# The GLA gate of a two-block fp32 kernel: tokens as the stationary operand, the bias as a rank-1 matmul, and four insertions moved

## The chip, the cores and the metric

The kernel runs on one core of one Trainium2 chip. The metric is the device time of one execution in microseconds (us); lower is better. TensorE (PE) has two rows in the profile, PE for matmuls and PEld for the loads of their stationary operand. VectorE is DVE, ScalarE is ACT, GpSimd is POOL and SyncE is SP.

## The reference, cut to what matters

The program is a stack of two blocks over 256 tokens of width 1024, all in fp32. The second block has two layers, and the change lies in the mixer of each of them. In a mixer the normed input is multiplied by `w_in`; 16 of the resulting columns, `p[..., o5:o6]`, are the input of a gate:

```python
h = rms_norm(x, norm_mix_g[l])
p = h @ w_in[l]
y_a = conformer_conv(p[..., :256], p[..., 256:512], ...)     # 31 taps
...
gate_logit = p[..., o5:o6] @ gla_gate_w[l] + gla_gate_b[l]   # [256, 16] @ [16, 256]
log_a = jax.nn.log_sigmoid(gate_logit) / 16.0
y_c = gla_chunked(q_c, k_c, v_c, log_a)                      # cumulative sums of log_a in chunks of 32
```

The convolution needs its own product, a sigmoid gate, a transpose to channels on partitions, and 31 taps for each of 2 channel tiles.

## The kernel before, in words

There are two token tiles of 128 (index m) and eight tiles of the width (index kt). All weights come as a stream of units of 128x2048 fp32 numbers through four slots. Each unit is split into two parts that TensorE can take at its fast rate: ACT writes the high part (`hi(U)`, L463, `whi<-raw`), DVE subtracts it and writes the low part (`lo(U)`, L872, `wlo`). The normed and transposed input is split likewise into `xth` and `xtl`. A product is then three matmuls (`split3`, L1404 to L1406). A slot comes free for the next DMA, which the SP queue issues, once `lo` of its unit is done, and `hi(U)` waits until TensorE has used unit U-4.

A mixer layer runs on TensorE as `step(0)` to `step(3)`, a half-width product (`mv`), `step(5)` and `out_product`. One step is for each m 24 matmuls of 512 columns (8 kt of 3). `step(1)` uses units U0+2 and U0+3, `step(2)` U0+4 and U0+5, `step(3)` U0+6 and U0+7; its second half of kt (kt 4 to 7) needs the second unit. Small work is inserted by hooks after a given kt of m=0 or m=1, or between the two (`end`). The order on each engine is written out by hand; engines wait on semaphores only.

The order around the change, between step 0 and step 3:

- **TensorE**: step 0; the gate product (24 matmuls, `ginh`/`ginl` stationary, `xth`/`xtl` of all 256 tokens moving, output 16x256, so already transposed); step 1 with `conv_turn` after kt 1 of m=0 (four transposes of `hc`, L1432) and `logits` after kt 3 of m=0 (L1749); step 2 with `cumsum` after kt 5 of m=0 (L1757) and `qk_turn` after kt 1 of m=1; step 3.
- **ACT**: sigmoid of the conv gate (L704), `gT` copy (L707), `hpad` copy (L711, from which the taps read), `hi(U0+4)`, then Abs, Exp and Ln of the logits (L717 to L721), `hi(U0+5)`, `gqk` (L727), `hi(U0+6)`, three reads of the cumulative sum (L737 to L739), `hi(U0+7)`.
- **DVE**: `hc` (L1165), two instructions that scale the logits and add the bias (L1169), taps 0 to 4 (L1185, L1189), `lo(U0+4)`, taps 5 to 8, the minimum and subtraction that finish `la` (L1199), `lo(U0+5)`, taps 9 to 13, `lo(U0+6)`, `dG` (L1208), `dec` (L1212), and so on to the last tap (41), the sum with POOL's part (L1262) and the seventh state (L1244).
- **POOL**: 20 taps of the second channel tile as product and sum (L431, L435), from `hpad` on.

Later on, TensorE waits for DVE twice in this layer by construction: the state products (L1789, `state_inc(n)`) need `state(n-2)`, and `ln_turn` (transposes of `cacc`) with the `gla_out` behind it needs the last tap and `state(6)`.

Of the kernel before, what the change touches and what calls it, by code (L numbers as in the profile page):

```python
# [77 lines left out]
def two_blocks_kernel(nc, x_in, stream, cols, bs_col, ws_t, gs_row, fin_row, fin2_row, rel_rows, ffn_cw,  # L78
                      conv_w, conv_ln, moba_g, gla_g, gate_w, gate_b, gate_in, out):
    ctx = ExitStack()  # L80
    with ctx:
        def sem(name):
            return ctx.enter_context(nc.semaphore(name))
# [3 lines left out]
        def at(name, shape, offset, dt=F32):  # L87
            return nc.alloc_sbuf_tensor_at(name, [P] + shape, dt, offset=base + 4 * offset)
# [26 lines left out]
        def const(name, shape, dt=F32):  # L115
# [69 lines left out]
        mqT = at("mqT", [2, SEQ], o_sa + 1792)  # L185
        mkT = at("mkT", [2, SEQ], o_sa + 2304)
        mv = at("mv", [M, 256], o_sa + 2816)
        gw_sb = at("gw_sb", [256], o_sb)
        gb_sb = at("gb_sb", [256], o_sb + 256)
        gin = at("gin", [KT * RANK], o_sb + 512)  # L190
# [41 lines left out]
        x_ltr, x_bn, x_ag, x_lms, x_lr, x_nrm, x_btr, x_sl = (  # L232
            sem("conv_ln_" + n) for n in ("transposed", "stats", "mean", "var", "rstd", "normed", "back", "silu"))
        x_ev = sem("mix_kept")
        x_gT, x_gTc, x_lg, x_z, x_ab, x_ex, x_ln, x_la, x_cs = (
            sem("gla_" + n) for n in ("gate_transposed", "gate_t_kept", "logit", "logit_scaled", "abs", "exp",
                                      "log", "log_a", "cumsum"))
        x_qktr, x_G, x_e1, x_gd, x_e2, x_qg, x_kd, x_kdtr, x_kdc = (
            sem("gla_" + n) for n in ("qk_transposed", "G_kept", "exp_G", "G_diff", "exp_diff", "q_decayed", "k_decayed",
# [95 lines left out]
        def _(pool):  # L335
# [77 lines left out]
            for l in range(2):  # L413

                pool.wait_ge(unit_used, gu(l))
                pool.dma_start(gw_sb[0:RANK, :], gate_w[l]).then_inc(x_ld, 16)
                pool.dma_start(gb_sb[:, :], gate_b[l].to_broadcast([P, 256])).then_inc(x_ld, 16)
                pool.dma_start(gin[:, :], gate_in[l]).then_inc(x_ld, 16)
                root(STATS[4 + 2 * l])
                pool.memset(hpad[:, :, 0:TAPS - 1], 0.0).then_inc(x_pad, 1)  # L420

                pool.wait_ge(n_lo, 4 * (4 + 2 * l) + 4)
                pool.wait_ge(n_sq, 2 * STATS[4 + 2 * l] + 2)
                pool.memset(aT[:, :, :], 0.0).then_inc(x_at0, 1)

                pool.wait_ge(x_cpad, l + 1)
                for i in range(POOL_TAPS):
                    dst = ptap if i else cacc2
                    if i > 1:
                        pool.wait_ge(x_pa, (POOL_TAPS - 1) * l + i - 1)  # L430
                    pool.tensor_scalar(dst[:, :], hpad[:, 1, i:i + SEQ], cw[:, l, 1, i:i + 1], None,  # L431
                                       ALU.mult).then_inc(x_pm, 1)
                    pool.wait_ge(x_pm, POOL_TAPS * l + i + 1)
                    if i:
                        pool.tensor_tensor(cacc2[:, :], cacc2[:, :], ptap[:, :], ALU.add).then_inc(x_pa, 1)  # L435

                pool.wait_ge(x_ag, 2 * l + 2)
                pool.tensor_scalar(stat[:, 72:74], mvv[:, :, 1], 1.0, LN_EPS, ALU.mult, ALU.add).then_inc(x_lms, 1)
                pool.wait_ge(x_lms, l + 1)
                pool.tensor_tensor(stat[:, 74:76], stat[:, 72:74], mhalf[:, 0:2], ALU.pow).then_inc(x_lr, 1)  # L440
                head_root(l, 0, DV)
                head_root(l, 1, DH)
                root(6 + 2 * l)
                if l == 1:
                    pool.wait_ge(f_lo, 2 * CTF)
                    pool.dma_start(frow[:, :], fin2_row.to_broadcast([P, D])).then_inc(f_row, 16)
                if l == 1:
                    final_root(FIN2, 1)
# [3 lines left out]
        def _(act):  # L452
# [237 lines left out]
            for l in range(2):  # L690
# [11 lines left out]
                for m in range(M):  # L702
                    wait_group(act, C0, U0 + 2, m)
                    act.activation(sgc[:, m, :], pair_bank(pair, m)[:, 256:512], ACT.Sigmoid,  # L704
                                   scale=rms(r, m)).then_inc(x_sig, 1)
                act.wait_ge(x_gT, l + 1)
                act.activation(gT[0:RANK, :], tb[0][0:RANK, 0:SEQ], ACT.Copy).then_inc(x_gTc, 1)  # L707

                act.wait_ge(x_ctr, l + 1)
                act.wait_ge(x_pad, l + 1)  # L710
                act.activation(hpad[:, :, TAPS - 1:TAPS - 1 + SEQ], tb[1][:, :].rearrange("p (a t) -> p a t", t=SEQ),  # L711
                               ACT.Copy).then_inc(x_cpad, 1)
                hi(U0 + 4)

                act.wait_ge(x_z, l + 1)
                tm = tmp[:, :, :].rearrange("p m c -> p (m c)")
                act.activation(tm, la[:, :, :].rearrange("p m c -> p (m c)"), ACT.Abs).then_inc(x_ab, 1)  # L717
                act.wait_ge(x_ab, l + 1)
                act.activation(tm, tm, ACT.Exp, scale=-1.0).then_inc(x_ex, 1)
                act.wait_ge(x_ex, l + 1)  # L720
                act.activation(tm, tm, ACT.Ln, bias=ones[:, 0:1]).then_inc(x_ln, 1)  # L721
                hi(U0 + 5)

                def keep(j, dst, n=512, func=ACT.Copy, tiles=range(M)):
                    for m in tiles:
# [139 lines left out]
        def _(dve):  # L865
# [287 lines left out]
            for l in range(2):  # L1153
# [9 lines left out]
                for m in range(M):  # L1163
                    dve.wait_ge(x_sig, 2 * l + m + 1)
                    dve.scalar_tensor_tensor(hc[:, m, :], pair_bank(pair, m)[:, 0:256], rms(r, m), sgc[:, m, :],  # L1165
                                             ALU.mult, ALU.mult).then_inc(x_gated, 1)
                dve.wait_ge(x_lg, l + 1)
                for m in range(M):
                    o = dve.scalar_tensor_tensor(la[:, m, :], tb[3][:, 256 * m:256 * m + 256], rms(r, m), gb_sb[:, :],  # L1169
                                                 ALU.mult, ALU.add)  # L1170
                o.then_inc(x_z, 1)

                first = [(0, i) for i in range(TAPS)]
                second = [(1, i) for i in range(POOL_TAPS, TAPS)]
# [4 lines left out]
                def taps(n0, n1):  # L1179
                    for a, i in order[n0:n1]:  # L1180
# [6 lines left out]
                        else:  # L1187
# [2 lines left out]
                                                     ALU.add).then_inc(done, 1)  # L1190

                dve.wait_ge(x_cpad, l + 1)
                taps(0, 5)
                lo(U0 + 4)
                taps(5, 9)

                dve.wait_ge(x_ln, l + 1)
                laf = la[:, :, :].rearrange("p m c -> p (m c)")
                dve.scalar_tensor_tensor(laf, laf, 0.0, tmp[:, :, :].rearrange("p m c -> p (m c)"), ALU.min,  # L1199
                                         ALU.subtract).then_inc(x_la, 1)  # L1200
                lo(U0 + 5)
                taps(9, 14)
                lo(U0 + 6)

# [197 lines left out]
        def _(pe):  # L1402
# [293 lines left out]
            for l in range(2):  # L1696
# [22 lines left out]
                step(0, m0={3: second_turns} if l == 0 else {})  # L1719

                pe.wait_ge(x_gl, l + 1)
                for kt in range(KT):
                    ws = slice(RANK * kt, RANK * kt + RANK)
                    mm = split3(tb[0][0:RANK, 0:SEQ], ginh[:, ws], ginl[:, ws], xth[:, kt, :], xtl[:, kt, :], kt == 0,
                                kt == KT - 1)
                mm.then_inc(x_gT, 1)

                def conv_turn():
                    for m in range(M):
                        pe.wait_ge(x_gated, 2 * l + m + 1)  # L1730
                        for a in range(2):
                            mm = turn(tb[1][:, a * SEQ + m * P:a * SEQ + (m + 1) * P], hc[:, m, a * P:(a + 1) * P])
                    mm.then_inc(x_ctr, 1)

                def qk_turn():

# [9 lines left out]
                def logits():  # L1746
                    pe.wait_ge(x_gTc, l + 1)
                    for m in range(M):
                        mm = pe.matmul(tb[3][:, 256 * m:256 * m + 256], gT[0:RANK, m * P:(m + 1) * P],  # L1749
                                       gw_sb[0:RANK, :], start=True, stop=True)  # L1750
                    mm.then_inc(x_lg, 1)

                def cumsum():
# [114 lines left out]
                            f(*a)  # L1868
                    return run

                step(1, m0={1: conv_turn, 3: logits})
                step(2, m0={5: cumsum}, m1={1: qk_turn})
                step(3, m0={5: kd_turn}, end=all_of((gla_scores, (0,)), (gla_scores, (1,))),
                     m1={5: lambda: state_inc(0)})
                state_inc(1)
# [176 lines left out]
```

## Time and profile before

| | before |
|---|---|
| median of 3 runs | 1305.81 us (1304.63 to 1306.94) |
| the profiled execution: its own time, and its span | 1305.81 us, 1304.0 us |
| PE busy, PEld busy | 1270.3 us (97%), 1038.2 us (80%) |
| DVE, ACT, POOL busy | 821.7 us (63%), 673.9 us (52%), 141.3 us (11%) |
| mean granted TensorE clock | 0.996 |

The span is the time from the first to the last instruction; what lies around it is 1.8 us. Matmul records overlap, so that how long TensorE takes is read from the distance of their starts and not from their durations. Engine busy shares are means over the whole program; for a change in one stage the order of time in that stage is what counts.

### The profile page before, as it was taken

Reading aid. Unit: us, or ns where it says so; the run is one execution under the profiler, and the core shown is the slowest. Engines: PE = TensorE matmul, PEld = TensorE weight load, DVE = VectorE, ACT = ScalarE, POOL = GpSimd, SP = SyncE. Lnnn points to the kernel's source line nnn. Section 1 sums busy time; section 2 is a strip of 40 time slices with the busy share of each in tenths; the row PEclk is TensorE's granted clock in tenths of the full one; section 3 lists DMA queues with packets and bytes.
Section 4 is the critical chain, followed back from the end, with each engine's and each line's share of the span. In section 5 each row is a group of like instructions: output and inputs, shape, how many; then the busy total and the mean of one; then the engine's idle time right before and its main releaser. Section 6 shows DMA issues by size and latency. Waiting matters only on the chain.

```text
span 1304.0 us, 16493 instructions
## 1 busy us (share of the span) xinstructions
PE 1270.3 (97%) x6160; PEld 1038.2 (80%) x6160; DVE 821.7 (63%) x983; ACT 673.9 (52%) x793; POOL 141.3 (11%) x166
## 2 busy tenths in 40 slices
PE   6999999999999999999989999999999999999997
PEld 5888888888887678888877777888888777888886
DVE  5466555554655556555458967777746987777762
ACT  6545364453455445444347365766635544776651
POOL 2000000000000000000017720000003941000000
PEclk9999999999999999999999999999999999999999
DMA  8544455546363325555624325455362433544440
GB/s 335 206 170 183 164 193 193 192 162 226 110 228 122 121 97 193 193 193 181 229 97 163 141 88 196 161 188 193 144 243 104 166 126 129 186 172 163 188 177 33
DMA packets 31526, 220.13 MB, mean 169 GB/s; under 512 B 3888, under 2 KB 3920, under 8 KB 5488
## 3 DMA queue, kind: packets, MB, share of 16 engines
q1 hardware_dynamic: 29664, 213.92, 44.3%
q0 software_dynamic: 1664, 5.41, 1.3%
q8 instruction: 39, 0.64, 0.2%
q14 instruction: 15, 0.12, 0.0%
q10 hardware_dynamic: 144, 0.04, 0.0%
HBM read 218.30 MB, written 1.05 MB: 168 GB/s over the span
## 4 chain that ended last, share of the span: by engine, by line
PE 92%; DVE 5%; ACT 1%; issue 1%; POOL 1%; DMA 0%; POOLq 0%; DVEq 0%; ACTq 0%
PE acc L1404 28%; PE acc L1406 27%; PE acc L1405 27%; PE tb L1432 5%; DVE wlo L872 2%; PE tb L1599 1%; PE tb L1598 1%; DVE cacc L1189 1%; PE tb L1789 1%; PE tb L1495 1%; PE tb L1815 0%; PE tb L1821 0%; ACT whi L463 0%; ACT junk L477 0%; POOL stat L407 0%
## 5 line engine op out<-in xcount | busy, mean ns | idle before, releaser
L872 DVE TENSOR_TENSOR wlo<-raw,whi 128x2048 fp32r<-128x2048 f32 x202 | 462.6, 2310 | 248.6 <-ACT whi L463 248.6
L1404 PE MATMUL acc<-whi,xth 128*128 128x512 f32 (+1 forms) x1088 | 432.5, 398 | 8.2 <-DVE wlo L872 6.1
L463 ACT ACTIVATE whi<-raw 128x2048 fp32r<-128x2048 f32 x202 | 380.2, 1907 | 101.9 <-PE acc L1406 100.9
L1406 PE MATMUL acc<-whi,xtl 128*128 128x512 f32 (+1 forms) x1088 | 422.6, 388 | 0.0
L1405 PE MATMUL acc<-wlo,xth 128*128 128x512 f32 (+1 forms) x1088 | 422.0, 388 | 0.0
L1404 PEld LDWEIGHTS acc<-whi,xth 128*128 128x128 f32 x1088 | 205.2, 189 | 53.8 <-issue 7.9
L1406 PEld LDWEIGHTS acc<-whi,xtl 128*128 128x128 f32 x1088 | 205.2, 189 | 42.6
L1405 PEld LDWEIGHTS acc<-wlo,xth 128*128 128x128 f32 x1088 | 205.6, 189 | 38.3
L1404 PE MATMUL acc<-whi,yth 128*128 128x512 f32 x544 | 217.2, 399 | 3.7 <-DVE ytl L1337 1.8
L1406 PE MATMUL acc<-whi,ytl 128*128 128x512 f32 x544 | 213.1, 392 | 0.0
L1405 PE MATMUL acc<-wlo,yth 128*128 128x512 f32 x544 | 212.7, 391 | 0.0
L1404 PEld LDWEIGHTS acc<-whi,yth 128*128 128x128 f32 x544 | 102.7, 189 | 27.7 <-issue 8.1
L1406 PEld LDWEIGHTS acc<-whi,ytl 128*128 128x128 f32 x544 | 102.5, 188 | 21.9
L1405 PEld LDWEIGHTS acc<-wlo,yth 128*128 128x128 f32 x544 | 102.7, 189 | 19.8
L1352 DVE SCALAR_TENSOR_TENSOR cv<-tb,fcw,cv 128x255 f32<-128x255 f32 (+1 forms) x176 | 72.7, 475 | 14.4 <-ACT cv L819 11.8
L979 DVE SCALAR_TENSOR_TENSOR yy<-acc,stat,sg 128x256 f32<-128x256 f32 x44 | 20.9, 480 | 80.5 <-ACT sg L558 80.5
L558 ACT ACTIVATE sg<-acc,stat 128x256 f32<-128x256 f32 x44 | 20.6, 472 | 88.8 <-PE acc L1406 88.7
L431 POOL TENSOR_SCALAR ptap<-hpad,cw 128x256 f32<-128x256 f32 x38 | 62.2, 1636 | 3.7
L468 ACT ACTIVATE xth<-xg 128x512 fp32r<-128x512 f32 x32 | 19.9, 631 | 79.6 <-DVE xg L882 79.4
L810 ACT ACTIVATE us<-acc,stat 128x512 f32<-128x512 f32 x44 | 30.5, 692 | 56.9 <-PE acc L1406 56.9
L1189 DVE SCALAR_TENSOR_TENSOR cacc<-hpad,cw,cacc 128x256 f32<-128x256 f32 x80 | 48.7, 639 | 1.0
L819 ACT ACTIVATE cv<-tb,fcw 128x256 f32<-128x256 f32 x88 | 42.4, 563 | 10.0 <-PE tb L1432 10.0
(217 smaller groups left out, 873.5 us busy)
## 6 DMA issues: line engine op xcount, KB each, us to landing
raw<-in_stream SPq DMA_DIRECT2D x202, 1024.0 KB, 4.8
rb<-in_rel_rows POOLq DMA_DIRECT2D x8, 256.0 KB, 3.0
x<-in_x_in SPq DMA_DIRECT2D x2, 512.0 KB, 5.1
gs_sb<-in_gs_row POOLq DMA_DIRECT2D x1, 1024.0 KB, 5.5
frow<-in_fin_row POOLq DMA_DIRECT2D x2, 512.0 KB, 5.0
out<-x SPq DMA_DIRECT2D x2, 512.0 KB, 2.6
ws_sb<-in_ws_t POOLq DMA_DIRECT2D x1, 512.0 KB, 4.2
gb_sb<-in_gate_b POOLq DMA_DIRECT2D x2, 128.0 KB, 3.0
```

The costliest lines, as they stand in the source:

```text
L431: pool.tensor_scalar(dst[:, :], hpad[:, 1, i:i + SEQ], cw[:, l, 1, i:i + 1], None, ALU.mult).then_inc(x_pm, 1)
L463: act.activation(whi[:, s, :], raw[:, s, :], ACT.Copy).then_inc(hi_ready, 1)
L810: act.activation(us[:, j % 2, m, :], pair_bank(j + pair, m)[:, :], ACT.Copy, scale=rms(r1, m)).then_inc(f_ev, 1)
L819: o = act.activation(cv[:, j % 2, a, :], tb[2 * (j % 2) + a // 2][:, (a % 2) * SEQ:(a % 2 + 1) * SEQ], ACT.Identity, scale=fcw[:, l, bass. ...
L872: dve.tensor_tensor(wlo[:, s, :], raw[:, s, :], whi[:, s, :], ALU.subtract).then_inc(lo_ready, 1)
L979: dve.scalar_tensor_tensor(yy[:, j % 2, m, :], pair_bank(j + pair, m)[:, 256:512], rms(STATS[k], m), sg[:, j % 2, m, :], ALU.mult, ALU.mul ...
L1189: dve.scalar_tensor_tensor(cacc[:, a, :], src, w, cacc[:, a, :], ALU.mult, ALU.add).then_inc(done, 1)
L1352: o = dve.scalar_tensor_tensor(dst, src, fcw[:, l, bass.ds(16 * j + 4 * a + tap + 32 * t, 1)], dst, ALU.mult, ALU.add)
L1404: pe.matmul(o, xh, wh, start=first, stop=False)
L1405: pe.matmul(o, xh, wl, start=False, stop=False)
L1406: return pe.matmul(o, xl, wh, start=False, stop=last)
L1432: return pe.transpose(o, i, ident[0:n, 0:n])
```

## The change

In each of the two mixer layers the gate product has its operands exchanged: for each m and kt, 128 tokens of `xth`/`xtl` are stationary and the 16 columns of `ginh`/`ginl` move, which makes 48 matmuls and an output of 128x16 per token tile. ACT copies it to a new tile `g16` with the norm's scale in two instructions. A new hook `gate_turn` transposes `g16` (two transposes), and ACT copies `gT` from there. `logits` gets a second matmul per m, `ones` (1x128) by `gb_sb` (1x256), which adds the bias in PSUM; the two DVE instructions that scaled and added are gone, and Abs and the minimum read the logits from PSUM. `gb_sb` is loaded for one partition instead of broadcast to 128.

The hooks move: `gate_turn` stands after kt 3 of step 1, m=0; `conv_turn` from after kt 1 to the end of m=0; `logits` from kt 3 of m=0 to kt 3 of m=1; `cumsum` from kt 5 to the end of step 2, m=0; `qk_turn` from kt 1 to kt 3 of m=1. On ACT `hi(U0+4)` comes before the `gT` copy and `hi(U0+5)` before Abs. On DVE `lo(U0+4)` and `lo(U0+5)` come before all taps.

```diff
@@ -185,6 +185,7 @@
         mqT = at("mqT", [2, SEQ], o_sa + 1792)
         mkT = at("mkT", [2, SEQ], o_sa + 2304)
         mv = at("mv", [M, 256], o_sa + 2816)
+        g16 = at("g16", [M, RANK], o_sa + 3328)
         gw_sb = at("gw_sb", [256], o_sb)
         gb_sb = at("gb_sb", [256], o_sb + 256)
         gin = at("gin", [KT * RANK], o_sb + 512)
@@ -232,8 +233,8 @@
         x_ltr, x_bn, x_ag, x_lms, x_lr, x_nrm, x_btr, x_sl = (
             sem("conv_ln_" + n) for n in ("transposed", "stats", "mean", "var", "rstd", "normed", "back", "silu"))
         x_ev = sem("mix_kept")
-        x_gT, x_gTc, x_lg, x_z, x_ab, x_ex, x_ln, x_la, x_cs = (
-            sem("gla_" + n) for n in ("gate_transposed", "gate_t_kept", "logit", "logit_scaled", "abs", "exp",
+        x_g16, x_g16c, x_gT, x_gTc, x_lg, x_ab, x_ex, x_ln, x_la, x_cs = (
+            sem("gla_" + n) for n in ("gate_in", "gate_kept", "gate_transposed", "gate_t_kept", "logit", "abs", "exp",
                                       "log", "log_a", "cumsum"))
         x_qktr, x_G, x_e1, x_gd, x_e2, x_qg, x_kd, x_kdtr, x_kdc = (
             sem("gla_" + n) for n in ("qk_transposed", "G_kept", "exp_G", "G_diff", "exp_diff", "q_decayed", "k_decayed",
@@ -414,7 +415,7 @@
 
                 pool.wait_ge(unit_used, gu(l))
                 pool.dma_start(gw_sb[0:RANK, :], gate_w[l]).then_inc(x_ld, 16)
-                pool.dma_start(gb_sb[:, :], gate_b[l].to_broadcast([P, 256])).then_inc(x_ld, 16)
+                pool.dma_start(gb_sb[0:1, :], gate_b[l]).then_inc(x_ld, 16)
                 pool.dma_start(gin[:, :], gate_in[l]).then_inc(x_ld, 16)
                 root(STATS[4 + 2 * l])
                 pool.memset(hpad[:, :, 0:TAPS - 1], 0.0).then_inc(x_pad, 1)
@@ -703,23 +704,27 @@
                     wait_group(act, C0, U0 + 2, m)
                     act.activation(sgc[:, m, :], pair_bank(pair, m)[:, 256:512], ACT.Sigmoid,
                                    scale=rms(r, m)).then_inc(x_sig, 1)
+                act.wait_ge(x_g16, l + 1)
+                for m in range(M):
+                    act.activation(g16[:, m, :], tb[0][:, RANK * m:RANK * m + RANK], ACT.Copy,
+                                   scale=rms(r, m)).then_inc(x_g16c, 1)
+                hi(U0 + 4)
                 act.wait_ge(x_gT, l + 1)
-                act.activation(gT[0:RANK, :], tb[0][0:RANK, 0:SEQ], ACT.Copy).then_inc(x_gTc, 1)
+                act.activation(gT[0:RANK, :], tb[2][0:RANK, 0:SEQ], ACT.Copy).then_inc(x_gTc, 1)
 
                 act.wait_ge(x_ctr, l + 1)
                 act.wait_ge(x_pad, l + 1)
                 act.activation(hpad[:, :, TAPS - 1:TAPS - 1 + SEQ], tb[1][:, :].rearrange("p (a t) -> p a t", t=SEQ),
                                ACT.Copy).then_inc(x_cpad, 1)
-                hi(U0 + 4)
-
-                act.wait_ge(x_z, l + 1)
+                hi(U0 + 5)
+
+                act.wait_ge(x_lg, l + 1)
                 tm = tmp[:, :, :].rearrange("p m c -> p (m c)")
-                act.activation(tm, la[:, :, :].rearrange("p m c -> p (m c)"), ACT.Abs).then_inc(x_ab, 1)
+                act.activation(tm, tb[3][:, :], ACT.Abs).then_inc(x_ab, 1)
                 act.wait_ge(x_ab, l + 1)
                 act.activation(tm, tm, ACT.Exp, scale=-1.0).then_inc(x_ex, 1)
                 act.wait_ge(x_ex, l + 1)
                 act.activation(tm, tm, ACT.Ln, bias=ones[:, 0:1]).then_inc(x_ln, 1)
-                hi(U0 + 5)
 
                 def keep(j, dst, n=512, func=ACT.Copy, tiles=range(M)):
                     for m in tiles:
@@ -1164,11 +1169,9 @@
                     dve.wait_ge(x_sig, 2 * l + m + 1)
                     dve.scalar_tensor_tensor(hc[:, m, :], pair_bank(pair, m)[:, 0:256], rms(r, m), sgc[:, m, :],
                                              ALU.mult, ALU.mult).then_inc(x_gated, 1)
-                dve.wait_ge(x_lg, l + 1)
-                for m in range(M):
-                    o = dve.scalar_tensor_tensor(la[:, m, :], tb[3][:, 256 * m:256 * m + 256], rms(r, m), gb_sb[:, :],
-                                                 ALU.mult, ALU.add)
-                o.then_inc(x_z, 1)
+                lo(U0 + 4)
+                lo(U0 + 5)
+
 
                 first = [(0, i) for i in range(TAPS)]
                 second = [(1, i) for i in range(POOL_TAPS, TAPS)]
@@ -1190,15 +1193,12 @@
                                                      ALU.add).then_inc(done, 1)
 
                 dve.wait_ge(x_cpad, l + 1)
-                taps(0, 5)
-                lo(U0 + 4)
-                taps(5, 9)
+                taps(0, 9)
 
                 dve.wait_ge(x_ln, l + 1)
-                laf = la[:, :, :].rearrange("p m c -> p (m c)")
-                dve.scalar_tensor_tensor(laf, laf, 0.0, tmp[:, :, :].rearrange("p m c -> p (m c)"), ALU.min,
+                dve.scalar_tensor_tensor(la[:, :, :].rearrange("p m c -> p (m c)"), tb[3][:, :], 0.0,
+                                         tmp[:, :, :].rearrange("p m c -> p (m c)"), ALU.min,
                                          ALU.subtract).then_inc(x_la, 1)
-                lo(U0 + 5)
                 taps(9, 14)
                 lo(U0 + 6)
 
@@ -1719,11 +1719,12 @@
                 step(0, m0={3: second_turns} if l == 0 else {})
 
                 pe.wait_ge(x_gl, l + 1)
-                for kt in range(KT):
-                    ws = slice(RANK * kt, RANK * kt + RANK)
-                    mm = split3(tb[0][0:RANK, 0:SEQ], ginh[:, ws], ginl[:, ws], xth[:, kt, :], xtl[:, kt, :], kt == 0,
-                                kt == KT - 1)
-                mm.then_inc(x_gT, 1)
+                for m in range(M):
+                    for kt in range(KT):
+                        ts, ws = slice(m * P, (m + 1) * P), slice(RANK * kt, RANK * kt + RANK)
+                        mm = split3(tb[0][:, RANK * m:RANK * m + RANK], xth[:, kt, ts], xtl[:, kt, ts], ginh[:, ws],
+                                    ginl[:, ws], kt == 0, kt == KT - 1)
+                mm.then_inc(x_g16, 1)
 
                 def conv_turn():
                     for m in range(M):
@@ -1731,6 +1732,12 @@
                         for a in range(2):
                             mm = turn(tb[1][:, a * SEQ + m * P:a * SEQ + (m + 1) * P], hc[:, m, a * P:(a + 1) * P])
                     mm.then_inc(x_ctr, 1)
+
+                def gate_turn():
+                    pe.wait_ge(x_g16c, 2 * l + 2)
+                    for m in range(M):
+                        mm = turn(tb[2][0:RANK, m * P:(m + 1) * P], g16[:, m, :])
+                    mm.then_inc(x_gT, 1)
 
                 def qk_turn():
 
@@ -1746,8 +1753,9 @@
                 def logits():
                     pe.wait_ge(x_gTc, l + 1)
                     for m in range(M):
-                        mm = pe.matmul(tb[3][:, 256 * m:256 * m + 256], gT[0:RANK, m * P:(m + 1) * P],
-                                       gw_sb[0:RANK, :], start=True, stop=True)
+                        o = tb[3][:, 256 * m:256 * m + 256]
+                        pe.matmul(o, gT[0:RANK, m * P:(m + 1) * P], gw_sb[0:RANK, :], start=True, stop=False)
+                        mm = pe.matmul(o, ones[0:1, :], gb_sb[0:1, :], start=False, stop=True)
                     mm.then_inc(x_lg, 1)
 
                 def cumsum():
@@ -1868,8 +1876,8 @@
                             f(*a)
                     return run
 
-                step(1, m0={1: conv_turn, 3: logits})
-                step(2, m0={5: cumsum}, m1={1: qk_turn})
+                step(1, m0={3: gate_turn}, end=conv_turn, m1={3: logits})
+                step(2, end=cumsum, m1={3: qk_turn})
                 step(3, m0={5: kd_turn}, end=all_of((gla_scores, (0,)), (gla_scores, (1,))),
                      m1={5: lambda: state_inc(0)})
                 state_inc(1)
```

## Rows read from the trace of the kernel before

**Rows 1.** The profile page: the chain that ended last; the costliest groups.

```profile
PE 92%; DVE 5%; ACT 1%; issue 1%; POOL 1%; DMA 0%; POOLq 0%; DVEq 0%; ACTq 0%
...
L1189 DVE SCALAR_TENSOR_TENSOR cacc<-hpad,cw,cacc 128x256 f32<-128x256 f32 x80 | 48.7, 639 | 1.0
```

**Rows 2.** Timeline of TensorE, first mixer layer: start us, length us, engine, line, operation.

```profile
685.29 0.28 PE L1404 MATMUL tb<-xth,ginh 128*16 128x256 f32 x1
...
688.11 0.40 PE L1404 MATMUL acc<-whi,xth 128*128 128x512 f32 x1
...
689.48 0.60 PE L1432 MATMUL tb<-ident,hc 128*128 128x128 f32 x4
...
690.16 0.39 PE L1405 MATMUL acc<-wlo,xth 128*128 128x512 f32 x1
...
691.41 1.13 PE L1749 MATMUL tb<-gw_sb,gT 16*128 16x256 f32 x4
```

**Rows 3.** Instructions of single tiles and lines: ns min/median/max, first and last start, forms.

```profile
L1404 PEld LDWEIGHTS tb<-xth,ginh x16: 93/94/95, 685.1 to 999.2; 128*16 128x16 f32 x16
...
L1749 PE MATMUL tb<-gw_sb,gT x8: 374/375/479, 691.4 to 1003.7; 16*128 16x256 f32 x8
...
L1619 PEld LDWEIGHTS tb<-mv,pt x8: 191/192/192, 757.5 to 775.6; 128*128 128x128 f32 x8
...
L1821 PE MATMUL tb<-st_g,eG x56: 268/281/294, 745.3 to 754.0; 64*32 64x128 f32 x56
```

**Rows 4.** Timeline of TensorE: the matmuls with the fewest moving columns and the smallest tiles.

```profile
745.32 0.42 PE L1821 MATMUL tb<-st_g,eG 64*32 64x128 f32 x6
...
757.56 0.39 PE L1619 MATMUL tb<-mv,pt 128*128 128x64 f32 x2
757.78 0.39 PE L1620 MATMUL tb<-mv,pt 128*128 128x64 f32 x2
```

**Rows 5.** Timeline of TensorE where it stands beside DVE, steps 2 to 5.

```profile
703.94 0.50 PE L1404 MATMUL acc<-whi,xth 128*128 128x512 f32 x1 [0.29 <-DVE wlo L872]
...
744.48 0.63 PE L1432 MATMUL tb<-ident,cacc 128*128 128x128 f32 x4
```

**Rows 6.** Timeline of DVE, the same stretch.

```profile
692.58 0.88 DVE L1169 SCALAR_TENSOR_TENSOR la<-tb,stat,gb_sb 128x256 f32<-128x256 f32 x2 [4.14 <-PE tb L1749]
...
695.83 2.28 DVE L872 TENSOR_TENSOR wlo<-raw,whi 128x2048 fp32r<-128x2048 f32 x1
...
701.07 2.82 DVE L872 TENSOR_TENSOR wlo<-raw,whi 128x2048 fp32r<-128x2048 f32 x1
...
743.91 0.42 DVE L1262 TENSOR_TENSOR cacc<-cacc,cacc 128x256 f32<-128x256 f32 x1
```

**Rows 7.** Timeline of ACT, the same stretch.

```profile
690.12 0.60 ACT L711 ACTIVATE hpad<-tb 128x512 f32<-128x512 f32 x1 [1.44 <-PE tb L1432]
...
693.49 0.63 ACT L717 ACTIVATE tmp<-la 128x512 f32<-128x512 f32 x1 [0.97 <-DVE la L1169]
...
698.01 1.90 ACT L463 ACTIVATE whi<-raw 128x2048 fp32r<-128x2048 f32 x1
...
708.94 0.59 ACT L739 ACTIVATE nG<-tb 128x512 f32<-128x512 f32 x1
```

**Rows 8.** Timeline of POOL: the first, a slow and the last instruction of its taps.

```profile
690.83 0.94 POOL L431 TENSOR_SCALAR cacc<-hpad,cw 128x256 f32<-128x256 f32 x1 [7.61 <-ACT hpad L711]
...
695.72 3.10 POOL L431 TENSOR_SCALAR ptap<-hpad,cw 128x256 f32<-128x256 f32 x1
...
741.95 0.72 POOL L435 TENSOR_TENSOR cacc<-cacc,ptap 128x256 f32<-128x256 f32 x1
```

**Rows 9.** Start of step 0 on TensorE, and one stretch of it (busy us by engine, PEclk, DMA).

```profile
671.83 0.47 PE L1404 MATMUL acc<-whi,xth 128*128 128x512 f32 x1 [2.02 <-DVE xtl L894]
...
676.25 1.03 PE L1432 MATMUL tb<-ident,x 128*128 128x128 f32 x8
...
673.00:674.00 1.00, 1.00 (x4) 0.81 (x3) 0.48 (x1) 0.00 (x0) 0.01 (x1) 0.50 0.45 90
```

## The prediction

> **What bounds the kernel now.** I read the page first, then the timelines of TensorE, DVE, ACT and POOL between the gate product and `ln_turn`, then single lines for prices. The chain that ended last is TensorE for 92% and DVE for 5% [rows 1]: every microsecond added to TensorE's own order counts unless it takes the place of a wait. The second thing to see is the timeline of DVE in a mixer layer: it idles 4.14 us before it touches the logits [rows 6] and then works without a gap up to the sum of the taps at 743.91. TensorE starts `ln_turn` at 744.48 [rows 5], right behind it. So two clocks run side by side from 692 to 744: TensorE's order and DVE's order, and the layer ends by the later. The other layer shows the same pattern some 311.5 us later (gate product at 999 in [rows 3]); I price one layer and double it.
>
> **TensorE's own order.** The distance of starts counts.
>
> - Gate product. The 24 matmuls take 688.11 - 685.29 = 2.82 us, 0.117 each, bound by 256 moving columns [rows 2]. Afterwards there are 48 with 16 columns and a stationary operand of 128 columns. No such matmul is in the trace. The nearest has the same stationary size and 64 columns: four records start within 757.56 and 757.78 plus as much again, two per 0.22, so 0.11 each [rows 4]. The loads say what sets it: 192 ns for 128 columns against 94 ns for 16 [rows 3], so a wide load is some 0.1 us longer, and it is now paid 48 times with too little streaming to lie behind. I take 0.11: 5.28 us, **+2.46**. Lower bound: the cheapest back-to-back records are those of `gla_out`, six in 0.42 us with 0.28 for one, (0.42 - 0.28)/5 = 0.028 apart [rows 3, 4]; 48 of them are 1.3 us, -1.5. They load 32 columns into small tiles, so this end is far. Upper bound: load and streaming one after the other, the streaming at the dearest price per column of the rows (0.25 us for 256 columns in the `logits` item below, 0.001 each, 0.016 for 16): 0.126 each, 6.05 us, +3.2.
> - `gate_turn`: two transposes. Four cost 690.16 - 689.48 less one ordinary matmul of (689.48 - 688.11)/6 = 0.228, so 0.45 [rows 2]; two are **+0.25**.
> - `logits`: two fp32 matmuls more, each two records of 256 columns. Four records span 1.13 us, of which 0.375 is the last one's length [rows 2, 3]: 0.25 from start to start, times four, **+1.0**. That only one row of the array is used does not shorten it: the present ones have 16 rows. Bounds 0.85 and 1.1.
> - The wait of 0.29 us for `wlo` in the middle of step 2 [rows 5] is for `lo(U0+5)`, which ran at 701.07 to 703.9 [rows 6]; it now comes before the taps and step 2 comes later. **-0.29**.
>
> Sum for TensorE alone: +3.4 us per layer. The transposes, the cumulative sum and `qk_turn` are only moved and cost the same elsewhere.
>
> **DVE's order.** Two things go: the two instructions on the logits (0.88 us) and, in part, the idle time ahead of them, into which `lo(U0+4)` fits. But the taps now wait for more. `conv_turn` moves from 689.48 behind the longer gate product (+2.46), behind `gate_turn` (+0.25) and behind 18 further matmuls (18 x 0.228 = 4.1): 696.3. `hpad` follows by 0.64 us as before (690.12 against 689.48 [rows 2, 7]), so 696.9, done 697.5. Only then does ACT take `hi(U0+5)` (1.9 us [rows 7]), 699.4, and DVE `lo(U0+5)` (2.3 to 2.8 us [rows 6]): the taps begin at about 701.9 instead of 693.5. The waiting instruction here is `lo(U0+5)`, and queued behind it are all 42 taps. Of the old work from 693.5 to 743.91 (50.4 us) the two `lo` (2.28 + 2.82) are already done: 45.3 are left. That ends at 747.2, +3.3.
>
> Two more waits on the way. Nine taps later (4.9 us) DVE wants Ln at 706.8. `logits` starts at 696.3 + 0.45 + 12 x 0.228 = 699.5 and takes 2.0 us and the latency: Abs at about 702.0, and Abs to the end of Ln is 693.49 to 698.1 = 4.6 us [rows 7], 706.6: just in time. Then `la` 0.6, five taps and `lo(U0+6)` 2.8, `dG` 0.6: with 14 taps at 7.9 us in all (0.6 each [rows 1], the first of each channel tile shorter) DVE reaches `dec` at 713.8. `dec` needs both exponentials, done at 709.5 before [rows 7]. `cumsum` is later by TensorE's +3.4 and by six matmuls (1.4): ready at 714.3, a wait of **0.5**. So the tap sum is at 743.91 + 3.3 + 0.5, about +3.9, and `state(6)` with it. TensorE's own +3.4 lies ahead of that, and it will wait for DVE some 0.5 us, at the state products or at `ln_turn`. From there to the end of the layer everything hangs on what precedes it. **+3.9 per layer.**
>
> **What costs nothing.** The two `g16` copies on ACT fall into idle time: ACT has nothing to do between the sigmoid and the gate product's end, and `gate_turn` comes 2.7 us after that end. If they took over 2.5 us, TensorE would wait. The DMA of `gb_sb` becomes 1 partition instead of 128, and nobody waits for it. POOL's taps start 6.8 us later too (690.83 to 697.6) and end at 742.7 before [rows 8]. One `lo` fewer falls beside them, and a product took 3.10 us beside a `lo` against 0.94 alone, so they end at 742.7 + 6.8 - 2.1 = 747.4; DVE wants the sum at 747.8. The cover is 0.4 us: each tenth more is a tenth on the layer.
>
> Sum: 2 x 3.9 = 7.8 us on the profiled execution's own 1305.81 us (span 1304.0 and 1.8 around it), which is also the median of the runs shown: **1313.6**.
>
> **A rule weighed against it.** The rows put the small matmul at 0.11 us. The Trainium skill, page "TensorE: Matmul & The Clock Gate", section "Back-to-back issue gap", has a table with about 60 cycles, or 25 ns, for 1 to 64 columns, and adds that this leaves out the load of weights. By the table alone the gate product would fall to some 1.2 us, and the total would be no slower than now; this is rival 2 below. The 64-column row speaks against the table here.
>
> **Rivals.**
>
> 1. *The clock falls during the gate product.* Where TensorE had stood idle for 2.02 us and done only transposes before, the granted clock was 0.50 at 673 to 674, which is 1.2 GHz, and 12 matmuls took 676.25 - 671.83 = 4.42 us instead of 2.74: 1.7 us lost [rows 9]. The new gate product is 5.3 us in which loads fill the array's time and columns move for a small part. If that counts as little work, the clock falls once in each layer, and since `conv_turn` lies behind it, both orders shift: +1.7, in all 2 x 5.6 = 11.2, 1317.0; if in one layer only, 1315.3. Against it: TensorE is never without an instruction there, and in the attention parts with short matmuls the clock stays full. The page named above says, in its part on the clock gate, that the clock is halved after little activity, and warns of thin matmuls; no row here shows whether a load counts as activity.
> 2. *The loads are hidden; not slower.* Place: the 48 matmuls. If they start 0.028 us apart, TensorE's sum is -1.5 + 0.25 + 1.0 - 0.29 = -0.5 per layer, the taps start 4 us earlier and DVE is at or ahead of its old time: 1304.8. It decides below about 0.05 us a matmul, where DVE's +3.9 falls by 48 x 0.06 to +1.0 and the total stays within 0.2%. For it: the lowest row of all; against it: every row with a load of 128 columns.
> 3. *A wait of DVE grows.* POOL's sum late by 1 us or Ln late by 1 us gives +1 per layer: 1315.6. For it: margins of 0.2 and 0.4 us; against it: DVE would itself come later by the `lo` estimate of 2.8.
> 4. *The added work is swallowed* by TensorE's later waits for the heads' chain, some 2 us a layer: 1309.6. Against it: those waits begin at TensorE's own matmuls and move with them.
>
> **How the numbers follow.** Forecast as summed 50% (own range 1311.5 to 1315.5: upper and lower prices of logits, 0.10 to 0.12 per small matmul); clock 25%; rival 3 10%; rival 2 in full 3%, in part (0.06 to 0.09 us a matmul, 1308.6 to 1311.5) 7%; rival 4 3%; something I have not seen that saves time 2%. The range 1310.8 to 1317.6 leaves out the full clock case with anything on top, most of rival 2 and rival 4. The upper bound of 0.126 us a matmul (+0.8 per layer, 1315.2) lies in it. A difference under 0.2% (2.6 us) can't be told from none: slower 0.93, same 0.04, faster 0.03.
>
> **What would show it.** Right: 48 gate matmuls 0.11 us apart, 5.3 us from first to last; `logits` eight records in 2 us; `hpad` near 696.9, the first tap near 702 and the tap sum near 747.8; no wait for `wlo` in step 2, and a new short wait of TensorE for DVE at L1789 or L1432 `cacc`; POOL's last sum just ahead of DVE's. Wrong: gate matmuls under 0.05 us apart; a granted clock of 0.50 behind 686; DVE idle for more than 1 us between its first tap and the sum; or an `hpad` much later than 697, since everything on DVE's side hangs on it.

## The result and the profile after

The changed kernel takes 1321.82 us (median of 4 runs, 1321.57 to 1323.25) against 1305.45 before, ratio 1.012 (95% interval 1.0104 to 1.0137). The profiled execution has a span of 1319.9 us. The forecast was 1313.6 with a range up to 1317.6: the direction is right, the rise of 16.4 us is twice the forecast 7.8, and the time is outside the range.

First the gate product on the timeline of TensorE, first mixer layer (start us, length us); it answers to [rows 2].

```profile
684.75 0.17 PE L1404 MATMUL tb<-ginh,xth 128*128 128x16 f32 x1
684.78 0.26 PE L1405 MATMUL tb<-ginl,xth 128*128 128x16 f32 x1
684.89 0.26 PE L1406 MATMUL tb<-ginh,xtl 128*128 128x16 f32 x1
...
688.91 0.36 PE L1406 MATMUL tb<-ginh,xtl 128*128 128x16 f32 x1
689.12 0.36 PE L1404 MATMUL tb<-ginh,xth 128*128 128x16 f32 x1
...
691.04 0.77 PE L1404 MATMUL acc<-whi,xth 128*128 128x512 f32 x1
691.61 0.63 PE L1405 MATMUL acc<-wlo,xth 128*128 128x512 f32 x1
692.04 0.63 PE L1406 MATMUL acc<-whi,xtl 128*128 128x512 f32 x1
...
696.06 0.38 PE L1432 MATMUL tb<-ident,g 128*16 128x128 f32 x2
```

The 48 starts are 0.11 us apart up to 688.91 and 0.21 apart from then on, for the last ten; the dense matmuls behind it start 0.43 apart instead of 0.23 [rows 2]. The windows of the same kernel (length, then busy us and count of PE, PEld, DVE, ACT and POOL, granted clock, DMA share, GB/s) say why: the clock is at 0.50, 1.2 GHz, from inside the gate product until most of the 12 dense matmuls behind it have run, in both layers.

```profile
685.60:689.00 3.40, 3.40 (x32) 3.40 (x32) 2.29 (x3) 0.92 (x3) 0.00 (x0) 0.99 0.79 294
689.00:692.40 3.40, 3.40 (x14) 3.18 (x14) 0.00 (x0) 1.18 (x3) 0.00 (x0) 0.50 0.80 320
...
696.00:699.40 3.40, 3.40 (x19) 2.75 (x18) 0.00 (x0) 0.37 (x1) 0.00 (x0) 1.00 0.69 229
1003.00:1006.40 3.40, 3.40 (x30) 3.28 (x28) 3.12 (x4) 1.75 (x3) 0.00 (x0) 1.00 0.54 178
1006.40:1009.80 3.40, 3.40 (x18) 3.40 (x18) 0.00 (x0) 0.00 (x0) 0.00 (x0) 0.50 1.03 424
...
1013.20:1016.60 3.40, 3.40 (x10) 2.43 (x9) 2.29 (x1) 0.49 (x1) 0.00 (x0) 0.50 0.00 0
1017.00:1020.40 3.40, 3.40 (x18) 2.83 (x17) 0.00 (x0) 0.58 (x2) 0.00 (x0) 1.00 0.91 308
```

PE is busy for the whole of each window: a full busy column does not show that the array is at full speed, and a mean clock of 0.989 over the span hides the two stretches. Then ACT and DVE, which answer to [rows 7] and [rows 6].

```profile
699.69 0.60 ACT L717 ACTIVATE hpad<-tb 128x512 f32<-128x512 f32 x1 [2.85 <-PE tb L1432]
700.18 1.91 ACT L464 ACTIVATE whi<-raw 128x2048 fp32r<-128x2048 f32 x1
```

```profile
693.49 2.29 DVE L877 TENSOR_TENSOR wlo<-raw,whi 128x2048 fp32r<-128x2048 f32 x1 [5.61 <-ACT whi L464]
702.13 2.29 DVE L877 TENSOR_TENSOR wlo<-raw,whi 128x2048 fp32r<-128x2048 f32 x1 [6.34 <-ACT whi L464]
...
709.73 0.68 DVE L1199 SCALAR_TENSOR_TENSOR la<-tb,tmp 128x512 f32<-128x512 f32 x1
...
750.71 0.42 DVE L1262 TENSOR_TENSOR cacc<-cacc,cacc 128x256 f32<-128x256 f32 x1
```

The chain of the prediction is there, link by link (`hpad`, then `hi(U0+5)`, then `lo(U0+5)`, then the taps), only later: `hpad` at 699.7 instead of the forecast 696.9, and the tap sum at 750.7 instead of 747.8. DVE's idle time of 4.14 us has become two of 5.61 and 6.34. Up to the tap sum TensorE waits for DVE once, at the third state product, and by as much in the second layer:

```profile
737.02 0.65 PE L1797 MATMUL tb<-gv,kdt 32*64 32x128 f32 x8 [0.45 <-DVE st_g L1242]
```

Measured by TensorE alone, the first layer went from 97.72 us (gate product at 685.29 to the first head transpose of L1432 `mo` at 783.01) to 105.10 (684.75 to 789.85), +7.38; the second from 97.72 (996.81 to 1094.53) to 106.68 (1003.65 to 1110.33), +8.96. The two make 16.3, the whole difference (16.4 us between the medians, 15.9 between the two spans). The forecast had +3.9 in each.

### The profile page after: what moved, and what is told of

It reads as the page before. It is cut to its first block, busy times and chain, and to the rows that moved or that the text cites. A ratio compares the mean times of both kernels' runs of the same rounds, so it can differ in the third digit from the quotient of the medians.

```text
span 1319.9 us, 16613 instructions
## 1 busy us (share of the span) xinstructions
PE 1285.5 (97%) x6220; PEld 1052.8 (80%) x6220; DVE 820.5 (62%) x979; ACT 674.6 (51%) x797; POOL 135.7 (10%) x166
## 4 chain that ended last, share of the span: by engine, by line
PE 90%; DVE 6%; ACT 2%; issue 1%; POOL 1%; DMA 0%; POOLq 0%; DVEq 0%; ACTq 0%
PE acc L1404 27%; PE acc L1406 26%; PE acc L1405 26%; PE tb L1432 5%; DVE wlo L877 2%; DVE cacc L1192 1%; PE tb L1599 1%; ACT whi L464 1%; PE tb L1598 1%; PE tb L1495 1%; PE tb L1823 0%; PE tb L1797 0%; PE tb L1829 0%; PE tb L1406 0%; PE tb L1405 0%
## 5 line engine op out<-in xcount | busy, mean ns | idle before, releaser
L432 POOL TENSOR_SCALAR ptap<-hpad,cw 128x256 f32<-128x256 f32 x38 | 49.7, 1309 | 3.7
```

## The experiments

Theory A: the prediction's two orders (TensorE's and DVE's, of which the later one counts), with their sum of about 8 us, hold, and the other 8 are the clock. Theory B: the time went into the moved insertions and the late taps, and the clock is beside the point. Each run is compared with the kernel before on its own chip, whose median was 1305.60 to 1305.78 us.

**move128: as many matmuls and loads, more columns moving.**

```diff
-ws = slice(RANK * kt, RANK * kt + RANK)
-mm = split3(tb[0][:, RANK * m:RANK * m + RANK], ...
+ws = slice(0, 128)
+mm = split3(tb[0][:, 128 * m:128 * m + 128], ...
```

> The changed kernel, but the 48 gate matmuls move 128 columns instead of 16 (the whole of the high or low part for every kt), so the gate's sixteen columns hold other sums than wanted; the number of matmuls, loads and their order are the same. In the trace of the changed kernel a gate matmul took 0.111 us, set by its load of 128 columns; 128 moving columns take no more than that. Theory A (the granted clock fell to 0.50 in the gate product because only 16 columns moved per load, and that cost 3.5 us in the first layer and about 5 in the second): the clock stays at 1.00 in both layers, gate matmuls stay at 0.11 us, time about 1313.6 (1312.5 to 1315), which is 7.8 above before. Theory B (the time went to the moved hooks and the late taps, the low clock is a side effect): no change against the changed kernel, about 1321.8.

Measured: 1314.07 us, ratio 1.0063 (1.0048 to 1.0078). The window over the gate product and the same places as before on TensorE and DVE:

```profile
685.00:690.50 5.50, 5.50 (x50) 5.50 (x49) 3.12 (x4) 1.76 (x4) 0.00 (x0) 1.00 0.75 280
```

```profile
696.10 0.60 PE L1432 MATMUL tb<-ident,hc 128*128 128x128 f32 x4
...
786.90 0.66 PE L1432 MATMUL tb<-ident,mo 128*128 128x128 f32 x4 [1.34 <-DVE mo L1330]
```

```profile
747.77 0.42 DVE L1262 TENSOR_TENSOR cacc<-cacc,cacc 128x256 f32<-128x256 f32 x1
```

The clock stays at 1.00 with the same 48 loads, one every 0.11 us. The layer takes 786.90 - 684.98 = 101.92 us, +4.2, and the second one 101.93; the tap sum is at 747.8. Theory B is out: the moves are all in this kernel, and 7.8 us are gone. The clock costs 1321.82 - 1314.07 = 7.8 us; by layer 7.38 - 4.20 = 3.2 and 8.96 - 4.20 = 4.8.

**move32: 32 columns.** The same edit with two kt of the gate's weights side by side and 32 output columns.

> The changed kernel with 32 moving columns in the gate product instead of 16 (the gate's columns hold the wanted sums in part), 48 matmuls and loads as before. A load takes 0.11 us either way. If the clock answers to how much moves per load, 32 columns are still little beside the 128 that kept it: it falls as in the changed kernel, 1318 to 1322. If any increase were enough: 1313.6 to 1314.5.

Measured: 1319.18 us (1317.68 to 1322.89), ratio 1.0097 (1.0082 to 1.0113). The clock fell in both layers of the profiled execution, the slowest of four, whose mean clocks were 0.987, 0.992, 0.992 and 0.991 (before: 0.996). So 32 columns did not keep the clock; between 32 and 128 nothing was run.

```profile
684.00:700.00 16.00, 16.00 (x84) 13.99 (x83) 7.56 (x5) 6.49 (x8) 0.04 (x1) 0.79 0.43 157
1003.00:1020.00 17.00, 17.00 (x81) 14.93 (x80) 6.74 (x5) 5.67 (x8) 0.00 (x0) 0.70 0.39 144
```

**spread and spread6: the same small matmuls among dense ones.** Both compute what the changed kernel computes; `spread` puts 12 gate matmuls after each of kt 0 to 3 of step 1, `spread6` six after each of kt 0 to 7, with the `gT` copy behind `hpad` on ACT.

```diff
-step(1, m0={3: gate_turn}, end=conv_turn, m1={3: logits})
+step(1, m0={0: gate_part(0), 1: gate_part(1), 2: gate_part(2), 3: gate_part(3), 5: gate_turn}, end=conv_turn,
+     m1={3: logits})                                                        # spread
+step(1, m0={i: gate_part(i) for i in range(8)}, end=conv_turn, m1={1: gate_turn, 3: logits})   # spread6
```

> The changed kernel with the same 48 matmuls of 16 columns, but in four groups of 12 after kt 0, 1, 2 and 3 of step 1 (m=0), between groups of three matmuls of 512 columns, and the transposes of the gate after kt 5. The computation is the same. conv_turn, and so hpad and the taps, come after the same amount of work of TensorE. Theory A: 1.3 us of small matmuls alternate with 0.7 us of dense ones; if it is the long stretch of small ones that brings the clock down, it stays at 1.00 and the time is about 1313.6; if two thirds of small work are already too much, it falls for a part of the 8 us and the time is 1315 to 1321. Theory B: about 1321.8.

> As spread, but the 48 small matmuls in eight groups of 6, one after each kt of m=0 of step 1, so that small and dense work take the same time (0.67 and 0.68 us) in turn; the gate's transposes after kt 1 of m=1, hi(U0+4) ahead of the g16 copies and the gT copy behind hpad. In spread (1.3 us small, 0.7 us dense) the clock fell in some executions and not in others, 1315.4 to 1325.5. If it is the density of small matmuls that brings the clock down: no fall in any execution, and the gT copy ahead of hi(U0+5) costs up to 1.2 us a layer: 1314 to 1316.5 in all executions. If any alternation of this kind is a gamble: again a spread of several us between executions.

Measured: `spread` 1319.75 us, and no single value is a fair summary: its four executions took 1315.39, 1315.57, 1323.92 and 1325.48, with mean clocks of 0.994, 0.995, 0.988 and 0.987. The profiled one, 1315.57, shows both cases at once: its first layer keeps the full clock, its second does not. The two slow ones lie above the 1321 expected at most, and above the changed kernel; only their mean clocks are on record, so why is open.

```profile
684.00:692.50 8.50, 8.39 (x60) 7.43 (x58) 3.73 (x4) 2.34 (x4) 0.00 (x0) 1.00 0.66 249
1006.00:1012.00 6.00, 6.00 (x34) 5.03 (x34) 0.73 (x1) 2.53 (x4) 0.00 (x0) 0.78 0.16 67
```

The fall there came only behind the small matmuls: the last one started at 1008.70, within each group they were 0.11 us apart, and dense ones started 0.43 apart from 1009.76 to about 1012.5. That layer took 1.57 us longer than the first (102.83 against 101.26).

`spread6` took 1315.52 (1314.93 to 1316.10), ratio 1.0073 (1.0058 to 1.0089), with a mean clock of 0.996 in all four. Its windows over both gate products:

```profile
684.00:700.00 16.00, 15.87 (x97) 13.44 (x96) 6.20 (x5) 7.11 (x10) 2.48 (x3) 1.00 0.54 198
1001.00:1017.00 16.00, 16.00 (x99) 13.80 (x98) 5.43 (x6) 6.71 (x9) 2.90 (x4) 1.00 0.53 197
```

So the 16-column matmuls do not bring the clock down by themselves: as 48 in a row they did in both profiled layers of the changed kernel, in groups of 12 in one of two, in groups of 6 in none. Smaller groups also mean a smaller share of small work, so these runs do not tell which of the two counts. At a full clock the change costs 9.9 us in this arrangement, 1.4 more than in `move128`; each of its layers has a wait that `move128` has not (here the first; who waited for whom; us in total, times, longest):

```profile
PE acc L1403 <- DVE wlo L876: 1.2, 1, 1.2
```

**moves: the new order on the kernel before.** The hooks, `hi` and `lo` as in the change; gate product, scale and bias as before.

```diff
-step(1, m0={1: conv_turn, 3: logits})
-step(2, m0={5: cumsum}, m1={1: qk_turn})
+step(1, end=conv_turn, m1={3: logits})
+step(2, end=cumsum, m1={3: qk_turn})
```

> The kernel before with only the order of the change: conv_turn at the end of m=0 of step 1, logits at kt 3 of m=1, cumsum at the end of m=0 of step 2, qk_turn at kt 3 of m=1, hi(U0+4) ahead of the gT copy, hi(U0+5) ahead of Abs, both lo ahead of the taps. Gate product, bias and scale as before. Theory A with the steps of the prediction: hpad 4.1 us later, first tap at +5.7, two lo fewer behind it (5.1), the 0.88 us on the logits back among the taps: DVE is 1.4 late at the sum of the taps, TensorE gains its 0.29: about +1.4 a layer, 1308.3 (1307 to 1309.5), clock at 1.00. Theory B: most of the loss is here, +8 or more, 1313 and above.

Measured: 1309.87 us, ratio 1.0032 (1.0021 to 1.0044), +4.3 instead of +2.8. A longer wait took the place of the one removed, in both layers (1.70 and 1.66):

```profile
717.47 0.50 PE L1403 MATMUL acc<-whi,xth 128*128 128x512 f32 x1 [1.70 <-DVE wlo L872]
```

The tap sum is at 745.43 with everything ahead of it 0.6 us earlier than before, so DVE is 2.1 us late where I had 1.4: it waits 0.48 + 5.43 us for the two units instead of 4.14. A wait of 0.29 us for `lo(U0+5)` was bought off with 1.70 for `lo(U0+7)` in step 3 and 0.46 more at the third state product. These make 1.9 of the 2.1 us by which each layer grew (97.72 to 99.85).

**conv_early, and the bias left out with and without it.** `conv_early` is `move128` with `conv_turn` back at kt 1 and taps 0 to 13 in one piece:

```diff
-step(1, m0={3: gate_turn}, end=conv_turn, m1={3: logits})
+step(1, m0={1: conv_turn, 3: gate_turn}, m1={3: logits})
...
-taps(0, 9)
+taps(0, 14)
```

> The kernel move128 (gate matmuls with 128 moving columns, 1314.1, clock at 1.00) with conv_turn put back to kt 1 of step 1 and all of taps 0 to 13 ahead of the minimum that finishes la. In move128 the first tap is at 701.4 and the tap sum at 747.8 with TensorE waiting 0.47 us at the third state product. Here ACT reaches hpad at about 694 (behind hi(U0+4) and gT), the first tap comes at about 698.7, 2.7 us earlier, and DVE ends 2.7 us earlier. Two orders, the later one counts: TensorE's own order is unchanged, so only its waits for DVE go, 0.5 to 0.9 us per layer: 1312.3 to 1313.1. Rival (the late taps cost what they are late): 2.7 per layer, 1308.7.

The other three leave out the second matmul of `logits` in the changed kernel (`nobias`), in `move128` (`wide_nobias`) and in `conv_early` (`early_nobias`):

```diff
-mm = pe.matmul(o, ones[0:1, :], gb_sb[0:1, :], start=False, stop=True)
```

> The changed kernel without the two matmuls of ones by gb_sb, so the gate's bias is left out. Two orders run side by side and the later one counts (the prediction's picture): TensorE waited 0.45 us at the third state product and about 0.3 at the transposes of cacc for DVE, so that 1.0 us less on TensorE per layer is worth 0 to 0.3 per layer: 1321 to 1321.8. Rival (TensorE's order alone counts): 1.0 per layer, 1319.8.

> move128 (1314.1, clock at 1.00) without the two bias matmuls; the bias is left out. In the run nobias the clock fell in a different measure from execution to execution and hid the answer; here it stays up. In move128 TensorE waits for DVE in the middle of the layer, so DVE's order governs there and the bias matmuls (0.87 us per layer in the trace of the changed kernel, against the 1.0 of the prediction) lie beside it: two orders give 0 to 0.4 us per layer, 1313.3 to 1314.1. TensorE's order alone would give 0.87 per layer, 1312.3.

> conv_early (1312.2, clock at 1.00) without the two bias matmuls; the bias is left out. In conv_early TensorE has no wait for DVE up to the tap sum, so its own order governs and each microsecond taken from it must show in full: 0.87 us per layer, 1310.4 (1310.0 to 1310.9). If the bias matmuls are hidden here too: 1312.2.

| | us | ratio (95% interval) |
|---|---|---|
| conv_early | 1312.17 | 1.0047 (1.0034 to 1.0061) |
| nobias | 1321.10 | 1.0117 (1.0101 to 1.0132) |
| wide_nobias | 1313.60 | 1.0059 (1.0045 to 1.0073) |
| early_nobias | 1311.69 | 1.0040 (1.0027 to 1.0054) |

`conv_early` gains 1.9 us on `move128`, not the 5.4 by which its taps were to come earlier: TensorE's order takes over. It has no wait for DVE up to the tap sum, and each layer is 3.24 us longer than before, against the +3.4 of the prediction for TensorE alone. DVE did not keep its lead either: counted from the gate product its first tap is 2.5 us earlier than in `move128`, its tap sum only 1.1, because it waits 0.83 us for `hi(U0+6)` and 1.51 at `dec` on the way. `nobias` is 0.7 below the changed kernel, with executions from 1317.7 to 1321.6 and clocks from 0.992 to 0.989, so its time says nothing by itself. `wide_nobias` gains 0.5, within the expected 0 to 0.8 and also within the spread of `move128` (1313.16 to 1315.28). Its trace says more: TensorE, 0.87 us earlier, now waits 0.81 for `lo(U0+7)` in step 3, where `move128` has no wait. `early_nobias` is a miss: it should have gained 1.7 and gained 0.5, with executions from 1310.71 to 1313.28. Its trace shows that DVE's waits came straight back, in both layers:

```profile
720.60 0.50 PE L1403 MATMUL acc<-whi,xth 128*128 128x512 f32 x1 [0.24 <-DVE wlo L877]
...
734.86 0.65 PE L1795 MATMUL tb<-gv,kdt 32*64 32x128 f32 x8 [0.46 <-DVE st_g L1241]
```

The two waits are 0.70 of the 0.87 us, and a layer became 0.15 shorter (100.96 to 100.81). In `conv_early` the two orders were only some tenths apart, so that TensorE could give up no more than that. The profiled execution is the slowest of the five, with a longer stretch of low clock than `conv_early` between 460 and 470 us (mean 0.77 against 0.89), far from the edit.

**early_units: only `hi` and `lo` moved.** The kernel before with `hi(U0+4)` ahead of the `gT` copy, `hi(U0+5)` ahead of Abs, `lo(U0+4)` in DVE's idle time and `lo(U0+5)` after tap 4.

```diff
+lo(U0 + 4)
 dve.wait_ge(x_lg, l + 1)
...
 taps(0, 5)
-lo(U0 + 4)
+lo(U0 + 5)
 taps(5, 9)
```

> The kernel before with one part of the change alone: hi(U0+4) ahead of the gT copy on ACT and hi(U0+5) ahead of Abs, lo(U0+4) in DVE's idle time ahead of the logits, lo(U0+5) after tap 4. The gate product, the bias and every hook stay. DVE's idle time of 4.14 us takes the 2.3 us of a lo, so DVE is about 2.2 us early from then on; TensorE's own order is unchanged and saves its waits only: 0.3 to 0.45 for wlo in step 2 and some 0.1 later. About 0.5 per layer, 1304.6 (1304.0 to 1305.4). If DVE's order alone set the layer's end it would be 2.2 per layer, 1301.2.

Measured: 1303.99 us (11 runs), ratio 0.9988 (0.9979 to 0.9997), 1.7 us below the kernel before where 1.0 was expected. It is the one part of the change that pays, and by little. A layer is 0.74 and 0.78 us shorter. TensorE's timeline has no wait for DVE left in the layer up to the tap sum, and DVE has time to spare:

```profile
691.58 0.87 DVE L1170 SCALAR_TENSOR_TENSOR la<-tb,stat,gb_sb 128x256 f32<-128x256 f32 x2 [1.39 <-PE tb L1749]
...
707.98 0.17 DVE L1212 COPY dec<-eG 128x16 f32<-128x16 f32 x1 [0.88 <-ACT nG L739]
...
741.85 0.42 DVE L1262 TENSOR_TENSOR cacc<-cacc,cacc 128x256 f32<-128x256 f32 x1
```

## Why the prediction was wrong

- **The step that failed** is that the sum took the full clock for granted: it priced the gate product and the dense matmuls behind it at 2.4 GHz and put the fall of the clock at nothing, as rival 1 with 25%. The runs showed a granted clock of 0.50 in both layers, 7.8 of the 16.4 us. The first reason against rival 1 was that TensorE would never be without an instruction there. That was no reason: the window 1006.40 to 1009.80 has PE and PEld busy throughout at 0.50. The second was that the clock stays full in the attention parts; but there the short matmuls stand among dense ones (27 matmuls in the 5 us from 755), as in `spread6`, and not 48 in a row. The Trainium skill, page "TensorE: Matmul & The Clock Gate", in its part on the clock gate, lets the clock follow how busy the array has been, and its warning of thin matmuls is about waits for DMA between them. The trace agrees that the work ahead decides, and shows a fall without any wait.
- **The price of the rival** was a fall worth 12 dense matmuls, 1.7 us a layer, 1317.0 in all [rows 9], so that the range up to 1317.6 held the rival at that price only. Measured it is 3.2 and 4.8 us. The low clock also slows the rest of the stretch in which it fell: in the first layer the last ten small matmuls came at 0.21 instead of 0.11 (1.0 us) and the 12 dense ones behind it took 696.06 - 691.04 = 5.0 instead of 2.7 us (2.3). In the second layer it fell earlier in the product: 23 small ones were slow (2.3 us), and the dense ones took 5.3 us (2.5).
- **The sum without the clock** came out at 8.5 us in `move128`, the forecast said 7.8. The small matmul is 0.111 us, 5.3 for 48. TensorE alone is +3.24 in `conv_early`, forecast +3.4. In `move128` `hpad` is at 696.7 (forecast 696.9), the first tap at 701.4 (701.9), the tap sum at 747.8 (747.8), and the wait of TensorE at the third state product 0.47 (some 0.5). Part of this is luck: in that execution the gate product began 0.31 us earlier than in the one priced, so that DVE's order is really 0.3 late, which is the +4.2 of a layer instead of +3.9. The wait of 0.5 at `dec` is one of 0.23 at the next instruction, and POOL ended 1.2 us ahead of DVE instead of 0.4, so rival 3 did not come. On DVE two steps took longer than before: the first tap of the two channel tiles 1.16 us instead of 0.73, and `dG` (L1208) 1.22 instead of 0.68; no run shows why.
- **The table of rival 2** (the Trainium skill, page "TensorE: Matmul & The Clock Gate", section "Back-to-back issue gap": 25 ns for few columns, the load of weights left out) is no price for matmuls that each bring a load of 128 columns: here they are 0.111 us apart. That the loads are hidden was rightly given 3%.
- **Bias, 1.0 us on TensorE,** is 0.87 in the trace. By the traces its removal made a layer 0.10 us shorter in `wide_nobias` and 0.15 in `early_nobias`. That it would not show in the total was in the two-orders picture; how close the second order followed in `conv_early` I had not worked out.
- **The removed wait of 0.29 us** did go. The prediction did not ask what the reorder does to `lo(U0+7)`: in `moves` TensorE waits 1.70 for it in step 3. In the changed kernel and in `move128` this wait is absent, but only just: without the 0.87 us of the bias it is back with 0.89 (`nobias`) and 0.81 (`wide_nobias`). So the later TensorE hides it, and the bias rides almost free on DVE's order.
- **The swallowing of rival 4** did not happen: L1432 `mo` waits 1.33 us before and 1.33 after.

What the runs add up to, by subtraction: order 4.3 us (`moves`), exchange and bias at a full clock 4.2 (8.5 - 4.3), clock 7.8. Open is why the clock falls at 32 columns and not at 128, where exactly between `spread` and `spread6` an arrangement becomes safe, which of the two, group length or share, decides, and why two identical layers of one execution differ.

## What to carry to other kernels

Exchanging the operands of a thin product turned its cost here from moving columns into loads, and a run of matmuls that mostly load can take the clock down for the dense work behind it as well: look at the granted clock over the stretch, not at the busy share. If such matmuls are needed, put few at a time between dense ones (six between three of 512 columns kept the clock here, twelve did not always), or let more columns move with each load where that costs no time (`move128`). And when two engines run side by side within tenths of a microsecond, moving work earlier on one is worth what the other one waited, so fill the idle time that exists (`early_units`), and before moving anything later ask which `lo` behind it becomes late (`moves`).

## What was unexpected of the hardware

- The granted clock fell to 0.50 while matmuls and loads were issued without a gap, one per 0.11 us, and came back only after 4.7 and 5.3 us of dense matmuls at half speed: 12 matmuls of 512 columns took 5.0 us in the first layer and 5.3 in the second.
- The time at 0.50 differed between two identical layers of one execution, 3.2 against 4.8 us lost, and between executions of one kernel: the changed kernel gave 1317.8 with a mean clock of 0.992 once, and 1321.1 to 1323.3 at 0.987 to 0.990 otherwise; `spread` gave 1315.4 to 1325.5. In the profiled execution of `spread` the clock fell in the second layer alone, and only when the dense matmuls had begun.
- 128 moving columns cost the same time as 16 here (0.11 us each) and kept the clock, so the wider matmul was the faster one, by 7.8 us in the program.
